# Inverting the chunk matrices of an RWKV-7 mixer on compact 32x32 blocks instead of 64x64 ones

## What is computed

```python
def step(state, inp):
    r_t, w_t, k_t, v_t, kk_t, a_t = inp
    sa = jnp.einsum('bhvk,bhk->bhv', state, -kk_t)
    state = (state * w_t[:, :, None, :]
             + sa[..., None] * (kk_t * a_t)[:, :, None, :]
             + v_t[..., None] * k_t[:, :, None, :])
    y_t = jnp.einsum('bhvk,bhk->bhv', state, r_t)
    return state, y_t
```

## Time and profile before

| | us |
|---|---|
| median of three runs | 2943.32 (2942.22 to 2951.57) |
| time of the profiled execution | 2941.55 |
| its span | 2939.7 |
| chunk stage in it, 834.5 to 1073.0 | 238.5 |

### The profile page before, as it was taken

One profiled execution on the slowest core, in us unless ns is written; L12 is line 12 of the kernel. 1 busy time (PEld: TensorE's weight loads), 2 busy tenths in 40 slices (PEclk: granted clock), 3 DMA queues, 4 the chain that ended last, 5 costly groups with the idle time before them and its releaser, 6 DMA issues.

```text
span 2939.7 us, 47500 instructions
## 1 busy us (share of the span) xinstructions
PE 2859.6 (97%) x18428; PEld 2310.2 (79%) x18428; DVE 1246.1 (42%) x1713; ACT 862.2 (29%) x1250; POOL 194.0 (7%) x224
## 2 busy tenths in 40 slices
PE   6999999999889999999999999999999999999997
PEld 4867777777579975888888888888888888888886
DVE  5354445554555543334332334223432234333544
ACT  4334343434322222332221222212221122233333
POOL 3000000000022311110000000000000000011110
PEclk7999999999889987999999999999999999999998
DMA  5443444344331122333333333333333333333333
GB/s 176 134 122 122 150 144 138 106 136 129 104 119 42 55 74 65 98 95 93 100 93 100 93 100 93 100 93 100 93 100 93 100 93 100 93 100 105 95 96 89
DMA packets 505237, 303.45 MB, mean 103 GB/s; under 512 B 23325, under 2 KB 483765, under 8 KB 504125
## 3 DMA queue, kind: packets, MB, share of 16 engines
q1 hardware_dynamic: 481021, 270.02, 31.6%
q10 hardware_dynamic: 18976, 14.71, 1.6%
q0 software_dynamic: 5152, 17.40, 1.5%
HBM read 265.79 MB, written 36.31 MB: 103 GB/s over the span
## 4 chain that ended last, share of the span: by engine, by line
issue 59%; PE 33%; POOL 4%; DVE 2%; DMA 1%; ACT 1%; SPq 0%; POOLq 0%; DVEq 0%; ACTq 0%
PE acc L525 6%; PE acc L527 6%; PE acc L526 6%; PE bank L665 4%; POOL sumsq L1526 2%; PE bank L599 1%; PE bank L586 1%; POOL nm L1557 1%; PE acc L665 1%; PE bank L615 1%; PE bank L625 1%; PE bank L592 1%; PE bank L673 1%; PE bank L674 1%; PE bank L783 0%
## 5 line engine op out<-in xcount | busy, mean ns | idle before, releaser
L1143 DVE TENSOR_TENSOR w_lo<-w_raw,w_hi 128x1024 fp32r<-128x1024 f32 (+1 forms) x422 | 515.7, 1222 | 1312.9 <-ACT w_hi L850 1311.7
L525 PE MATMUL acc<-a_hi,w_hi 128*128 128x512 f32 x2080 | 826.3, 397 | 5.2 <-DVE a_lo L1410 5.0
L850 ACT ACTIVATE w_hi<-w_raw 128x1024 fp32r<-128x1024 f32 x420 | 445.2, 1060 | 1302.7 <-PE acc L527 1283.1
L526 PE MATMUL acc<-a_lo,w_hi 128*128 128x512 f32 x2080 | 816.5, 393 | 0.0
L527 PE MATMUL acc<-a_hi,w_lo 128*128 128x512 f32 x2080 | 816.5, 393 | 0.0
L525 PE MATMUL acc<-b_hi,w_hi 128*128 128x512 f32 x1280 | 498.5, 389 | 0.0
L526 PE MATMUL acc<-b_lo,w_hi 128*128 128x512 f32 x1280 | 498.0, 389 | 0.0
L527 PE MATMUL acc<-b_hi,w_lo 128*128 128x512 f32 x1280 | 498.0, 389 | 0.0
L525 PEld LDWEIGHTS acc<-a_hi,w_hi 128*128 128x128 f32 x2080 | 394.7, 190 | 100.4 <-issue 12.9
L527 PEld LDWEIGHTS acc<-a_hi,w_lo 128*128 128x128 f32 x2080 | 394.4, 190 | 83.2
L526 PEld LDWEIGHTS acc<-a_lo,w_hi 128*128 128x128 f32 x2080 | 394.9, 190 | 82.6 <-issue 1.9
(11 more groups left out here) (272 smaller groups left out, 2245.2 us busy)
## 6 DMA issues: line engine op xcount, KB each, us to landing
w_raw<-in_w_ff SPq DMA_DIRECT2D x256, 512.0 KB, 3.9
w_raw<-in_w_in SPq DMA_DIRECT2D x100, 512.0 KB, 3.6
w_raw<-in_w_out SPq DMA_DIRECT2D x32, 512.0 KB, 3.8
w_raw<-in_w_ple_gate SPq DMA_DIRECT2D x32, 512.0 KB, 3.8
z_d<-ev POOLq DMA_DIRECT2D x50, 256.0 KB, 3.2
ab_d<-ab ACTq DMA_DIRECT2D x8, 1024.0 KB, 4.7
x<-ab_d SPq DMA_DIRECT2D x8, 1024.0 KB, 4.8
xin<-in_x SPq DMA_DIRECT2D x16, 256.0 KB, 2.7
```

Source lines behind the costliest of these rows:

```text
L525: mm(dst, wh, hi[:, kt, :], start=kt == 0, stop=False)
L526: mm(dst, wh, lo[:, kt, :], start=False, stop=False)
L850: A(w_hi[:, s, :, :], w_raw[:, s, :, :], ACT.Copy).then_inc(sg("w_hi_ready"), 1)
L1143: V.tensor_tensor(w_lo[:, s, :, 0:width], w_raw[:, s, :, 0:width], w_hi[:, s, :, 0:width].bitcast(F32), ALU.subtract).then_inc(sg("w_split ...
```

## The change

The 64x64 matrices are split in halves of B = 32 tokens. Only their two diagonal 32x32 blocks are inverted by levels (now 1 to 4); these blocks are stored compactly, so that `xs`, `xt`, `nm` have 32 columns for a pair, and each group of a level makes 16 calls (`blocks`) on four 32x32 tiles on the array's diagonal, where `each` made 8 on two. PE also computes the two diagonal blocks of the product a second time, plain and transposed (`diagonals`, 64 calls), in place of the transpose for `xt`; the first product group shrinks from 128 to 64 columns. Identity is added on DVE before the product (`qt`), so that DVE sums nothing any more and ACT copies `xt` and `xs` out of PSUM. The fifth level becomes two small products for the upper right block: `ax`, and then `xb`, and `sa` is made of an upper and a lower part. POOL masks all eight pairs in one instruction a level.

```diff
+    j1, t1 = (p % B)[:, None], np.arange(B)[None, :]
+    for n in range(5):
         b = 1 << n
-        c[:, C_LVL + n * C:C_LVL + (n + 1) * C] = (
-(j[:, None] // (2 * b) == t[None, :] // (2 * b)) & (j[:, None] % (2 * b) < b) & (t[None, :] % (2 * b) >= b))
+        c[:, C_LVL + n * B:C_LVL + (n + 1) * B] = (j1 // (2 * b) == t1 // (2 * b)) & (j1 % (2 * b) < b) & (t1 % (2 * b) >= b)
+    c[:, C_LVT:C_LVT + B] = (j1 == t1 + 1) & (j1 % 2 == 1)
+    c[:, C_EYE1:C_EYE1 + B] = j1 == t1
...
-    gb = sb("gb", [P, NPAIR, 2, C], at)
+    gb = sb("gb", [P, NPAIR, C], at)
     gk = sb("gk", [P, NPAIR, 2, C], at)
-    nm = sb("nm", [P, 5, NPAIR, C], at)
-    xs = sb("xs", [P, 2, NPAIR, C], at)
-    xt = sb("xt", [P, NPAIR, C], at)
-    pt = sb("pt", [P, NPAIR, C], at)
+    nd = sb("nd", [P, NPAIR, B], at)
+    nb = sb("nb", [P, NPAIR, B], at)
+    nm = sb("nm", [P, 4, NPAIR, B], at)
+    xs = sb("xs", [P, 2, NPAIR, B], at)
+    xt = sb("xt", [P, NPAIR, B], at)
+    qt = sb("qt", [P, NPAIR, B], at)
+    ax = sb("ax", [P, NPAIR, B], at)
+    xb = sb("xb", [P, NPAIR, B], at)
...
-    for k in range(2):
-        for g in range(2):
-            each(g, gbank[g][k][:, :], lambda ph, n: x[ph, n, 2 + k, :], lambda ph, n: x[ph, n, 0:2, :].rearrange("p a t -> p (a t)"), "products_done")
+    def part(k):
+        return slice(k * B, (k + 1) * B)
+    def blocks(g, dst, lhs, rhs):
+        for n in range(g * H, (g + 1) * H):
+            for k in range(2):
+                for ph in range(2):
+                    r = slice(ph * HD + k * B, ph * HD + (k + 1) * B)
+                    last = mm(dst[r, n % H, :], lhs(r, n), rhs(r, n), start=True, stop=True)
+        return last
+    for g in range(2):
+        each(g, gbank[g][0][:, 0:H * C], lambda ph, n: x[ph, n, 2, :], lambda ph, n: x[ph, n, 1, :], "gram_done")
+        for at, one, two in ((2, 2, 0), (3, 0, 2)):
+            for n in range(g * H, (g + 1) * H):
+                for k in range(2):
+                    for ph in range(2):
+                        r = slice(ph * HD + k * B, ph * HD + (k + 1) * B)
+                        last = mm(block(g, 0, at)[r, n % H, :], x[heads[ph], n, one, part(k)], x[heads[ph], n, two, part(k)], start=True, stop=True)
+        last.then_inc(sg("diagonals_done"), 1)
+    for g in range(2):
+        each(g, gbank[g][1][:, :], lambda ph, n: x[ph, n, 3, :], lambda ph, n: x[ph, n, 0:2, :].rearrange("p a t -> p (a t)"), "products_done")
     for g in range(2):
         wait("state_ready", g, 1, 1)
+        for n in range(g * H, (g + 1) * H):
+            for ph in heads:
+                mm(block(g, 2, 2)[ph, n % H, :], x[ph, n, 2, :], x[ph, n, 0, part(1)], start=True, stop=True)
         each(g, gbank[g][2][:, 0:H * C], lambda ph, n: x[ph, n, 2, :], lambda ph, n: eye2[ph, :], "transposes_done")
     for g in range(2):
         wait("y_taken", g, 1, 1)
         each(g, gbank[g][3][:, 0:H * C], lambda ph, n: x[ph, n, 3, :], lambda ph, n: eye2[ph, :], "transposes_done")
     for g in range(2):
-        wait("products_ready", g, 2, 1)
+        wait("gram_ready", g, 1, 1)
+        wait("nd_taken", g, 1, 1)
+        wait("xt0_ready", g, 1, 1)
         each(g, gbank[g][0][:, 0:H * C], lambda ph, n: v[ph, n, :], lambda ph, n: eye2[ph, :], "transposes_done")
-    for g in range(2):
-        wait("products_ready", g, 2, 2)
-        wait("x_ready", g, 6, 1)
-        each(g, gbank[g][1][:, 0:H * C], lambda ph, n: xs[ph, 0, n, :], lambda ph, n: eye2[ph, :], "xt0_done")
-    for lv in range(1, 6):
+    for lv in range(1, 5):
         old = (lv - 1) % 2
         for g in range(2):
-            wait("n_ready", g, 5, lv)
-            wait("xt_ready", g, 5, lv)
-            each(g, gbank[g][1][:, 0:H * C], lambda ph, n: nm[ph, lv - 1, n, :], lambda ph, n: xt[ph, n, :], "pt_done")
+            if lv == 1:
+                wait("products_ready", g, 1, 1)
+            else:
+                wait("xt_ready", g, 4, lv - 1)
+            pe.wait_ge(sg("n_ready"), 4 * c + lv)
+            blocks(g, block(g, 1), lambda r, n: nm[r, lv - 1, n, :], lambda r, n: xt[r, n, :]).then_inc(sg("pt_done"), 1)
         for g in range(2):
-            wait("pt_ready", g, 5, lv)
-            wait("x_ready", g, 6, lv)
-            if lv < 5:
-                if lv == 1:
-                    wait("transposes_taken", g, 3, 2)
-                each(g, gbank[g][3][:, 0:H * C], lambda ph, n: xs[ph, old, n, :], lambda ph, n: pt[ph, n, :], "dxt_done")
+            wait("q_ready", g, 4, lv)
             if lv == 1:
-                wait("transposes_taken", g, 3, 1)
-            each(g, gbank[g][2][:, 0:H * C], lambda ph, n: pt[ph, n, :], lambda ph, n: xs[ph, old, n, :], "dx_done")
+                wait("transposes_taken", g, 3, 2)
+            else:
+                wait("x_ready", g, 4, lv - 1)
+            blocks(g, block(g, 3), lambda r, n: xs[r, old, n, :], lambda r, n: qt[r, n, :]).then_inc(sg("xt_done"), 1)
+            if lv == 1:
+                wait("nb_taken", g, 1, 1)
+            blocks(g, block(g, 2), lambda r, n: qt[r, n, :], lambda r, n: xs[r, old, n, :]).then_inc(sg("x_done"), 1)
+    upper, lower = (slice(0, B), slice(HD, HD + B)), (slice(B, HD), slice(HD + B, P))
+    for g in range(2):
+        wait("xt_ready", g, 4, 4)
+        for n in range(g * H, (g + 1) * H):
+            for up, lo in zip(upper, lower):
+                last = mm(block(g, 1)[lo, n % H, :], nb[up, n, :], xt[up, n, :], start=True, stop=True)
+        last.then_inc(sg("ax_done"), 1)
     for g in range(2):
         wait("transposes_taken", g, 3, 3)
         wait("state_ready", g, 1, 1)
         both(g, gbank[g][0][:, 0:H * C], lambda ph, n: (x[ph, n, 0, :], state[ph, n, :]),
              lambda ph, n: (gk[ph, n, 0, :], vt[ph, n, :])).then_inc(sg("r_done"), 1)
+    for g in range(2):
+        wait("x_ready", g, 4, 4)
+        pe.wait_ge(sg("xb_copied"), 2 * c + 2)
+        pe.wait_ge(sg("ax_ready"), 4 * c + 2 * g + 2)
+        for n in range(g * H, (g + 1) * H):
+            for up, lo in zip(upper, lower):
+                last = mm(block(g, 2)[up, n % H, :], ax[lo, n, :], xs[lo, 0, n, :], start=True, stop=True)
+        last.then_inc(sg("x12_done"), 1)
     for g in range(2):
         wait("r_ready", g, 1, 1)
-        wait("x_ready", g, 6, 6)
-        each(g, gbank[g][1][:, 0:H * C], lambda ph, n: xs[ph, 1, n, :], lambda ph, n: rr[ph, n, :], "sa_done")
+        for n in range(g * H, (g + 1) * H):
+            for up in upper:
+                mm(half(g, 1)[up, n % H, :], xs[up, 0, n, :], rr[up, n, :], start=True, stop=True)
+        pe.wait_ge(sg("xb_ready"), 4 * c + 2 * g + 2)
+        for n in range(g * H, (g + 1) * H):
+            for ph, lo in zip(heads, lower):
+                last = mm(half(g, 1)[lo, n % H, :], xb[ph, n, :], rr[ph, n, :], start=True, stop=True)
+        last.then_inc(sg("sa_done"), 1)
...
+    for g in range(2):
+        wait("diagonals_done", g, 1, 1)
+        A(nd[:, pairs[g], :], block(g, 0, 2), ACT.Copy).then_inc(sg("nd_taken"), 1)
     transposed(0)
+    for g in range(2):
+        A(nb[:, pairs[g], :], block(g, 2, 2), ACT.Copy).then_inc(sg("nb_taken"), 1)
     transposed(1)
-    for lv in range(1, 6):
+    for lv in range(1, 5):
         for g in range(2):
-            wait("pt_done", g, 5, lv)
-            A(pt[:, pairs[g], :], half(g, 1), ACT.Copy).then_inc(sg("pt_ready"), 1)
+            wait("xt_done", g, 4, lv)
+            A(xt[:, pairs[g], :], block(g, 3), ACT.Copy).then_inc(sg("xt_ready"), 1)
+            wait("x_done", g, 4, lv)
+            A(xs[:, lv % 2, pairs[g], :], block(g, 2), ACT.Copy).then_inc(sg("x_ready"), 1)
         if lv == 1:
             transposed(2)
+    for g in range(2):
+        wait("ax_done", g, 1, 1)
+        for lo in (slice(B, HD), slice(HD + B, P)):
+            A(ax[lo, pairs[g], :], block(g, 1, 0, lo), ACT.Copy).then_inc(sg("ax_ready"), 1)
+    for g in range(2):
+        wait("x12_done", g, 1, 1)
+        for up in (slice(0, B), slice(HD, HD + B)):
+            A(xb[up, pairs[g], :], block(g, 2, 0, up), ACT.Copy).then_inc(sg("xb_ready"), 1)
...
+    def ones(g, dst, src):
+        return V.tensor_tensor(dst, src, const(C_EYE1, B)[:, None, :].broadcast_to([P, H, B]), ALU.add)
+    def level0(g, dst, at, mask, name):
+        V.tensor_tensor(dst, block(g, 0, at), const(mask, B)[:, None, :].broadcast_to([P, H, B]), ALU.mult).then_inc(sg(name + "_masked"), 1)
+    for g in range(2):
+        wait("nd_taken", g, 1, 1)
+        level0(g, xs[:, 0, pairs[g], :], 2, C_LVL, "x0")
+        level0(g, xt[:, pairs[g], :], 3, C_LVT, "xt0")
+    for g in range(2):
+        wait("gram_done", g, 1, 1)
+        V.tensor_tensor(gb[:, pairs[g], :], half(g, 0), const(C_MASK + C, C)[:, None, :].broadcast_to([P, H, C]), ALU.mult).then_inc(sg("gram_ready"), 1)
+    for g in range(2):
+        wait("x0_masked", g, 1, 1)
+        ones(g, xs[:, 0, pairs[g], :], xs[:, 0, pairs[g], :]).then_inc(sg("x0_ready"), 1)
+        wait("xt0_masked", g, 1, 1)
```

(83 more changed lines are left out.)

1 line of the change is left out of this document (added).

## The result

After the change the kernel takes 3063.33 us (median of 4 runs, 3055.92 to 3067.60), against 2943.95 us of the kernel before beside it (4 runs): ratio 1.0408, interval 1.0393 to 1.0422. That is 119 us more, where 95 were forecast. The profiled execution took 3055.92 us, its span 3054.2.

What follows compares the result with a forecast made beforehand. PE's array work bounds the kernel before, instruction fetching the changed chunk stage: 83 us from eight longer chunks plus 12 for the clock, 95 on the profiled 2941.55, median 1.8 above, gives 3038 us; range 2975 to 3135.

Steps and rivals of the forecast that it cites:

- Where the bound is now: Chunk stage before the change: PE bounds it, busy 29.56 of 29.70 us a chunk, so only its list counts.
- The new bound: Chunk stage after: instruction fetching, one packet ahead, 3.45 us per 256 instructions; 11.3 packets a chunk, 39.1 us.
- The cost of a small call: 32x32 calls in the chunk stage: between 14.6 ns and 58.3 ns of array work each, thought nearer the lower end.
- The rival of 58.3 ns a call: Chunk stage: a small matmul costs PE what a large one does, +14.0 us a chunk, 3055 us; chance 0.12.
- the estimate by the Trainium skill: Small calls in the chunk stage: floor of about 25 ns between matmuls, giving 39.5 us a chunk; no separate chance.
- The clock, in the straight parts of a chunk: `r`, `s`, `y` and next products begin at half clock after the levels: 1.5 us a chunk, 12 us in all.
- between 0 and 3.1 I take the middle: Clock loss in dense parts after the levels: at most 3.1 us a chunk, taken as 1.5 us.
- What other engines hide: Levels: ACT, DVE and POOL work hides behind a level's 5.2 us of fetching; fewer POOL and DVE instructions gain nothing.
- The sentence on what would be late without the cover of fetching: Levels: without fetching's cover, the round PE, DVE, PE, ACT, put below 2 us, would be late.
- Fetching isn't the limit: Rival: levels are a round of waits, 4 x 1.9 us, 23.1 us a chunk, 2890 us; chance 0.18.
- The clock staying at half: Rival: clock stays at half for the whole chunk stage, +23.7 us a chunk, 3133 us; chance 0.07.

Runs made afterwards that it cites:

- the looped version of before: Kernel before with its first four 64x64 levels as one hardware-looped body, masks and inverse in one buffer each: 2950.45 us, ratio 1.0017.
- a looped turn at full clock: Compact kernel with looped levels, plus blocks copied instead of multiplied again and `sa` one call a head, against the kernel before: 2967.39 us, 1.0074.
- the last two runs: Kernel before with looped levels, plus 5 or 10 small 32x32 calls ahead of each level group: 3022.58 us (1.0275) and 3041.13 us (1.0338).
- the looped kernel: Kernel after with TensorE's four levels as one body run by a hardware loop, masks and inverse in one buffer each: 2974.65 us, 1.0096 to before.

## Why the prediction was right in kind and short by a fifth in size

- **Where the bound is now.** Put: PE's own array work, 29.56 of 29.70 us. Right: the looped version of before has 2.25 packets a chunk less to fetch and is 0.2% off.
- **The new bound.** Put: fetching, one packet ahead, 3.45 us for 256 instructions. Right in kind, shown by the loop (89 us back with the same calls executed), by the stops in the middle of groups, and by the count: some 91 packets forecast, 90 found. In the levels also right in size: 1536 instructions are 6 packets, 20.7 us by the forecast, and 20.7 us is the mean of the eight that were measured.
- **The cost of a small call.** Taken near the lower bound of 14.6 ns. Right, at 17 to 20 ns: in a looped turn at full clock a group of 16 calls starts 0.32 us after the one before (950.92, 951.24), 20 ns a call, and each further call in the last two runs is 17 ns. The rival of 58.3 ns a call falls with that. So does the estimate by the Trainium skill (TensorE: Matmul & The Clock Gate, on the back-to-back gap): small matmuls on different tiles of the array start on average 8 to 10 ns apart here, below the page's floor of about 25 ns.
- **The term that was mis-sized.** The clock, in the straight parts of a chunk. Put: 1366 instructions, 5.3 packets at 3.45 (18.4 us), 0.6 for dense stretches, 0.5 for a wait, together 19.5 us; and 1.5 for the clock. Put together 21.0 us; the measured means are 13.1 us (back) and 10.6 (front), 23.7. The 2.7 us that are missing, eight times, are 22 of the 24 us between forecast and result. At full clock and with hardly a stop the same instructions took 10.32 us in the back part (the looped kernel) and 8.35 in the front part (the shortest of the seven in after), 18.7 us. Of the 5.0 us above that, 3.1 are PE busy for longer (means 12.6 and 9.2 us, against 10.3 and 8.4), nearly all of it in parts where the clock is below 1.00: the half clock lasts for 3 to 14 us of a back part. So the step "between 0 and 3.1 I take the middle" was mis-sized, and the upper bound was what came. The other 1.9 us are stops by "issue" in the straight parts, where the sum had fetching at 3.45 us a packet and hardly more. They are not the clock's alone; a front part of after at full clock has the longest:

```profile
1060.62:1072.37 11.75, 8.59 (x338) 1.00 0.33 114
...
1067.67 0.92 PE L677 MATMUL acc<-x 64*64 64x128 f32 x13 [3.16 <-issue]
```

  The operands of a later chunk are loaded beside six of the seven front parts (106 to 148 GB/s), and the seventh has no stop; but the looped kernel has one of 1.42 us in a front part without such a load (1074.73 to 1084.79, 5 GB/s). What delays these packets stays open. Nothing hangs on a slip in the working: a packet of level calls needs 0.93 us of the array by the lower bound (64 calls), not 1.05.
- **What other engines hide.** Right in after, where VectorE and ScalarE wait for PE. The sentence on what would be late without the cover of fetching was right in naming the round and wrong in its size: with PE's own part it is 2.77 us, not 1.9. The rival "Fetching isn't the limit" had 2890 us by that 1.9; the looped kernel, which fetches next to nothing in three of four turns, still takes 2974.65.
- **The clock staying at half.** It did not; the stage alternates, and the half clock (0.5, the lower of its two levels) comes where PE pauses between bursts, in the levels, and reaches into the dense parts: 999.04 to 1003.18, the 64 matmuls of `r`, is at 0.50 and takes 4.14 us; the looped kernel takes 2.06 us for them at 1.00.

## What to carry to other kernels

Cutting a matmul into smaller tiles buys array time with instructions; where a stage is written out straight, compare instructions against packets (here 256 in 3.4 to 3.6 us, 13.5 ns an instruction, against 14.6 ns that a 64x64 call needs for each of its four) before counting the array's gain. If it can't be avoided, put the repeated part in a hardware loop whose body stays: that gave back 89 of 119 us. Then look at what the shorter work uncovers: the round of copies between the products, and the clock, which fell here when PE paused in the levels (0.58 to 0.66 over them) and was still low in the dense part behind.

## What the runs showed that was not expected

- A looped body of some 390 instructions was executed three times in a row without one instruction packet for PE (952.8 to 962.2 us), but its first turn stopped for 1.88 us, and two of its three turns back show about 0.3 us of "issue".
- Small 32x32 calls between 64x64 ones cost some 0.24 us for going over and back, 14 times the 17 ns of a further call, without any idle time put down to it: PE shows as busy through it.
- A level on compact blocks with nothing fetched takes 2.77 us, a 64x64 level 3.03 us, with half the columns and twice the tiles at once. The array's part fell from 2.8 us (48 calls at 58.3 ns) to 1.9 (96 at 20), and copies took up all but 0.26 of the gain.
